# A tenth home for expert weight tiles, five experts a loop turn, earlier loads and a reordered first gather in a single-core MoE step

## The reference

```python
def moe_ffn(h, w_router, b_router, w_gu, b_gu, w_down, b_down):
    logits = h @ w_router + b_router              # 320 x 32
    top_val, top_idx = top_k(logits, 4)           # 4 of 32 experts a row
    gate = softmax(top_val)
    for e in range(32):                           # rows that chose expert e
        gu = x_e @ w_gu[e] + b_gu[e]              # w_gu[e]: 1024 x 2048 float32, 8 MiB
        gt, up = min(gu[:, :1024], 7), clip(gu[:, 1024:], -7, 7)
        act = gt * sigmoid(1.702 * gt) * (up + 1)
        y[rows] += gate * (act @ w_down[e] + b_down[e])   # w_down[e]: 1024 x 1024, 4 MiB
```

## Time and profile before

| | |
|---|---|
| median of 3 runs | 1288.66 us (1286.66 to 1289.59) |
| the profiled execution | 1286.78 us |
| its span, first to last instruction | 1285.0 us |
| PE busy | 98% of the span, 8556 matmul records |
| DVE, ACT busy | 36%, 16% |
| mean granted PE clock | 0.995 of full speed |
| read from HBM | 435 MB |

### The profile page before, as it was taken

The page is one execution under the profiler, slowest core; times in us unless marked ns, Lnnn a source line. Parts: engine busy times, 40 slices in busy tenths (PEclk is TensorE's granted clock), DMA queues, the critical chain, the costliest instruction groups (busy, mean ns, idle before and its releaser), DMA issues.

```text
span 1285.0 us, 20897 instructions
## 1 busy us (share of the span) xinstructions
PE 1254.3 (98%) x8556; PEld 574.0 (45%) x8556; DVE 459.5 (36%) x970; ACT 207.8 (16%) x547; POOL 18.2 (1%) x34
## 2 busy tenths in 40 slices
PE   8999999999999999999999999999999999999997
PEld 5677654576653333333333333343333334333332
DVE  4454334525572223333322332332232333222233
ACT  2542433623420000000000000000000000000000
POOL 0000001100000000000000000000000000000000
PEclk9999999999989999999999999999999999999999
DMA  9611011953089999999999999999999999999996
GB/s 311 254 66 67 2 30 26 322 251 145 4 358 429 427 426 430 427 429 427 429 427 429 427 429 428 429 428 429 428 429 427 429 427 429 427 429 427 430 427 266
DMA packets 48768, 439.06 MB, mean 342 GB/s; under 512 B 8677, under 2 KB 11213, under 8 KB 24058
## 3 DMA queue, kind: packets, MB, share of 16 engines
q1 hardware_dynamic: 48492, 438.32, 81.9%
q10 hardware_dynamic: 238, 0.20, 0.1%
HBM read 435.17 MB, written 3.33 MB: 341 GB/s over the span
## 4 chain that ended last, share of the span: by engine, by line
PE 80%; DMA 16%; ACT 1%; DVE 1%; issue 1%; SPq 0%; DVEq 0%; POOLq 0%; POOL 0%; ACTq 0%
PE bank L1092 78%; DMA weights<-in_w_gu 16%; PE bank L1095 2%; ACT scaled L639 1%; DMA x<-in_x_sample 1%; PE bank L1755 0%; DVE x L2509 0%; ACT weights L639 0%; ACT small_weights L639 0%; DVE scaled L1970 0%; ACT scaled L1020 0%; DVE x L2180 0%; DVE stats L2284 0%; DVE small_weights L2361 0%; DVEq L2545 0%
## 5 line engine op out<-in xcount | busy, mean ns | idle before, releaser
L2509 DVE SCALAR_TENSOR_TENSOR x<-bank,small_weights,x 128x512 f32<-128x512 f32 (+1 forms) x192 | 134.9, 744 | 598.5 <-PE bank L1092 598.5
L1092 PE MATMUL bank<-weights,small_weights 128*64 128x512 f32 x1360 | 308.7, 596 | 3.6 <-DMA weights<-in_w_gu 3.1
L1092 PEld LDWEIGHTS bank<-weights,small_weights 128*64 128x64 f32 x1360 | 92.4, 136 | 188.8 <-issue 170.2
L1092 PE MATMUL bank<-weights,scaled 128*64 128x512 f32 x704 | 155.9, 595 | 5.1 <-ACT scaled L639 5.1
L1092 PE MATMUL bank<-small_weights,weights 128*128 128x320 f32 (+4 forms) x400 | 110.0, 422 | 0.1
L1092 PE MATMUL bank<-scaled,small_weights 64*128 64x512 f32 x384 | 108.1, 640 | 1.4 <-DVE x L2509 0.7
L639 ACT ACTIVATE scaled<-scaled 128x512 f32<-128x512 f32 x32 | 20.1, 630 | 548.8 <-DVE scaled L1901 548.8
L639 ACT ACTIVATE scaled<-bank 128x512 f32<-128x512 f32 (+6 forms) x145 | 54.8, 406 | 325.8 <-PE bank L1092 244.7
L1092 PEld LDWEIGHTS bank<-weights,scaled 128*64 128x64 f32 x704 | 48.7, 137 | 97.1 <-issue 87.7
L1092 PE MATMUL bank<-stream,small_weights 128*64 128x512 f32 (+4 forms) x408 | 87.4, 544 | 1.5 <-DMA stream<-in_w_gu 1.1
L1092 PEld LDWEIGHTS bank<-stream 128*128 128x128 bf16 (+1 forms) x2416 | 75.0, 100 | 27.6 <-issue 26.4
(11 more groups left out here) (207 smaller groups left out, 879.8 us busy)
## 6 DMA issues: line engine op xcount, KB each, us to landing
weights<-in_w_gu SPq DMA_DIRECT2D x85, 2048.0 KB, 26.9
weights<-in_w_down SPq DMA_DIRECT2D x44, 2048.0 KB, 28.3
stream<-in_w_gu SPq DMA_DIRECT2D x21, 2048.0 KB, 28.1
more_weights<-in_w_gu SPq DMA_DIRECT2D x11, 2048.0 KB, 27.6
small_weights<-in_w_gu SPq DMA_DIRECT2D x11, 2048.0 KB, 26.2
small_weights<-in_w_down SPq DMA_DIRECT2D x10, 2048.0 KB, 28.2
more_weights<-in_w_down SPq DMA_DIRECT2D x10, 2048.0 KB, 28.4
weights<-in_w_in SPq DMA_DIRECT2D x3, 2048.0 KB, 14.0
```

Of the source, the lines that this page charges most:

```text
L1092: return pe.matmul(out, lhsT, rhs, start=start, stop=stop)
L2509: dve.scalar_tensor_tensor(xx, PS[bank][0:rows, :], gcur[0:rows, b:b + 1], xx, ALU.mult, ALU.add)\
```

## The change

- **Homes.** `SLOTN` becomes 10: two homes in `stream` (columns 3840 and 7936) in place of one, which takes smaller parts and tables there. 30 tiles are three times 10 homes, so `TURN` becomes 5, with six turns in place of ten.
- **Sample rows folded.** Block 2 of the residual is kept as `x3s`, 128 partitions x 512: partitions 0 to 63 hold the first half of the 64 rows, 64 to 127 the second. Its `x3_add`, its square, its parts, its `scatter` and its `accumulate` are one step of 512 columns in place of two half-filled ones (`HALVES` = 5 in place of 6 everywhere). A row's sum of squares then lies in two partitions; `sample_sum` (PE) adds them and `sample_rstd` (ACT) makes the norm. The router and the ranks of block 2 are computed for both halves of the partitions. A gather is 48 matmuls of 64 columns and 12 of 128.
- **Tables moved.** Masks, ranks, S and the lists move from `stream` to `small_weights`; the down bias to `gain_rows`; the raw bias, the router's weights and the small bfloat16 constants to `x`; the transposed rows for the router get a tile of their own, `x3T`; the memory attention's output `om` is split by row block.
- **First loads.** Four homes get their first tile on other conditions; the down bias is loaded and split with the gate-up bias.
- **The way to the first gather.** `x3_scale` goes: ACT makes the first part from `x3` with the norm as its scale, and `x3_rest` is a scale and subtract in one (two instructions). Masks are bfloat16, rank matmuls too. The ranks of blocks 0 and 1 have a bank and a mark (`rank01_mm`) of their own, `iota` starts at 1 so that one DVE operation less follows the ranks, and `slots` is two operations, `slots01` and `slots2`. `first_gather` does the 48 matmuls of blocks 0 and 1 when `slots01` is there, and block 2's afterwards. Gate sums are taken for all blocks at once.

The diff, cut to these parts:

```diff
@@ constants and homes
-        GT, TILES, SLOTN, TURN = 4, 6, 9, 3
-        slot_sb = [W[:, 4 * FF * n:4 * FF * (n + 1)] for n in range(6)] + [VK[:, 5888:9984], RH[:, 2816:6912], W2[:, :]]
+        GT, TILES, SLOTN, TURN = 4, 6, 10, 5
+        slot_sb = [W[:, 4 * FF * n:4 * FF * (n + 1)] for n in range(6)] + [VK[:, 3840:7936], RH[:, 2816:6912], W2[:, :], VK[:, 7936:12032]]
...
+        x3s, xs3s = X[:, 2 * D:2 * D + 512], XS[:, 2 * D:2 * D + 512]
+        HALVES = 2 * TB - 1
@@ SP
             for n in range(3):
                 load(braw[32 * n:32 * n + 32, :], b_gu[0], "ld_bias")
+            for n in range(3):
+                load(bdn[32 * n:32 * n + 32, :], b_down[0], "ld_bias")
...
             sp.wait_ge(sem("x2_mm"), KD)
+            first_tiles(TILES, TILES + 1)
+            sp.wait_ge(sem("x2_add"), KD)
+            first_tiles(8, 9)
+            sp.wait_ge(sem("b3_step"), 12)
             load(wr_sb, k_major(w_router[0], 0, KD), "ld_wr")
-            for n in range(3):
-                load(bdn[32 * n:32 * n + 32, :], b_down[0], "ld_wr")
-            sp.wait_ge(sem("x2_add"), KD)
-            first_tiles(SLOTN - 1, SLOTN)
             sp.wait_ge(*at("qm_mm"))
             first_tiles(0, 1)
-            sp.wait_ge(sem("x3_mm"), 2 * TB)
+            sp.wait_ge(sem("att_s"), ATT["mem"] + UNITS)
+            first_tiles(7, 8)
+            sp.wait_ge(sem("x3_mm"), HALVES)
             first_tiles(1, 2)
-            first_tiles(TILES, TILES + 1)
             sp.wait_ge(sem("lg_mm"), TB)
-            first_tiles(TILES + 1, SLOTN - 1)
+            first_tiles(9, 10)
@@ ACT
             def part(b, i):
-                act.wait_ge(sem("xs_ready"), 2 * b + i + 1)
-                run(xparts[:, b, i, :], xs3[:, b, :]).then_inc(sem("x3_part"), 1)
+                if i == 0:
+                    act.wait_ge(sem("x3_rstd"), 2 * b + 2)
+                    dst, src = (xparts[:, b, 0, :], x3[:, b, :]) if b < 2 else (sparts[:, 0, :], x3s)
+                    m = run(dst.rearrange("p (m i t) -> p m i t", i=2, t=P), src.rearrange("p (m t i) -> p m i t", t=P, i=2),
+                            scale=ssq[:, 8 + b:9 + b])
...
@@ PE
+            def sample_sum():
+                pe.wait_ge(sem("x3_sq"), TB)
+                for side in range(2):
+                    m = mm(PS[5][half(side), 0:1], eye2, ssq[:, 10:11])
+                m.then_inc(mark("pair_mm"), 1)
...
             rows_feature_major(2)
+            sample_sum()
             router(2)
...
             pe.wait_ge(*at("mask01_ready"))
-            for b, a in ((0, 0), (1, 0), (1, 1), (2, 0), (2, 1)):
-                ranks(b, a)
+            mm(PS[3][:, E:2 * E], onesb, mask[:, 0, :], True, False)
+            mm(PS[3][:, 0:E], ustrictb, mask[:, 0, :], False, False)
+            mm(PS[3][:, E:2 * E], ustrictb, mask[:, 1, :], False, True).then_inc(mark("rank01_mm"), 1)
+            for b in range(2):
+                mm(PS[6][:, 0:2 * E].rearrange("p (b e) -> p b e", b=2), onesb, bcast(mask[:, b, :], [P, 2, E], 1), b == 0, False)
             for b in range(2):
                 counts(b)
+            pe.wait_ge(sem("b3_step"), 12)
+            gate_up_bias(0)
             pe.wait_ge(*at("mask_ready"))
-            ranks(2, 2).then_inc(mark("rank_mm"), 1)
+            mm(PS[6][:, 0:2 * E], ustrictb, mask[:, 2:4, :], False, True).then_inc(mark("rank_mm"), 1)
...
                 pe.wait_ge(sem("slots_ready"), 1)
                 pe.wait_ge(sem("x3_part"), 4)
-                pe.wait_ge(sem("parts_ready"), 1)
-                gather_pass([(0, 0), (0, 1), (0, 2), (1, 0), (1, 1)], True, False)
+                pe.wait_ge(sem("parts_ready"), 2)
+                gather_pass(ALL_PARTS[0:6], True, False)
+                pe.wait_ge(sem("slots_ready"), 2)
                 pe.wait_ge(sem("x3_part"), 6)
-                gather_pass([(2, 0), (2, 1)], False, False)
+                gather_pass(ALL_PARTS[6:8], False, False)
                 pe.wait_ge(sem("parts_ready"), TB)
-                gather_pass([(1, 2), (2, 2)], False, True).then_inc(sem("gather_mm"), 1)
+                gather_pass(ALL_PARTS[8:9], False, True).then_inc(sem("gather_mm"), 1)
...
+                if b == 2:
+                    mm(PS[bank][:, :], slotT[:, 2 * P:3 * P], y_sb).then_inc(sem("scat_mm"), 1)
+                    return
@@ DVE
-            slots(0, None)
-            last_part(1)
+            dve.wait_ge(*at("rank01_mm"))
+            slot_ranks(0, 3)
+            slots01(0, iota[:, 0:SLOTS])
+            dve.wait_ge(*at("rank_mm"))
+            slot_ranks(2, 6)
+            slots2(0, iota[:, 0:SLOTS])
+            x3_rest(2)
```

More of the change, by code:

```diff
@@ L1061, in _ @@
             for b in range(TB):
-                rows = P if b < 2 else DEC
-                run(gate[0:rows, b, :], lg[0:rows, b, 0:E], ACT.Exp, bias=ntop[0:rows, b:b + 1]).then_inc(sem("gate_exp"), 1)
+                run(gate[:, b, :], lg[:, b, 0:E], ACT.Exp, bias=ntop[:, b:b + 1]).then_inc(sem("gate_exp"), 1)
             def sigmoid(it):
@@ L1685, in router @@
                         pe.wait_ge(sem("x3_ev"), 2 * b + 1 + k // 4)
-                    m = mm(PS[b][0:rows, 0:E], hT[:, k, b * P:b * P + rows], wr_sb[:, k, :], k == 0, k == KD - 1)
+                    if b < 2:
+                        m = mm(PS[b][:, 0:E], x3T[:, k, :], wr_sb[:, k, :], k == 0, k == KD - 1)
+                    else:
+                        for side in range(2):
+                            m = mm(PS[2][half(side), 0:E], x3T[:, k, 0:DEC], wr_sb[:, k, :], k == 0, k == KD - 1)
                 m.then_inc(sem("lg_mm"), 1)
@@ L1733, in gather_pass @@
             def gather_pass(terms, begin, end):
[L1735 removed]
+                for k in range(4):
                     for b, i in terms:
[L1737 to L1738 removed]
+                        first, last = begin and k == 0 and (b, i) == terms[0], end and k == 3 and (b, i) == terms[-1]
+                        if b == 2:
+                            m = mm(xg_pair[:, :, k, :], sparts[:, i, k * P:(k + 1) * P], S[:, 2, :, :], False, last)
+                            continue
+                        for kk in (k, k + 4):
+                            m = mm(PS[4][:, kk * SLOTS:(kk + 1) * SLOTS], xparts[:, b, i, kk * P:(kk + 1) * P], S[:, b, 0, :],
+                                   first and kk == k, last and kk > k)
                 return m
@@ L2447, in gates @@
             def gates():
                 dve.wait_ge(sem("gate_exp"), TB)
-                link(tt(gate, gate, mask, ALU.mult))
-                for b in range(TB):
-                    rows = P if b < 2 else DEC
-                    link(dve.tensor_reduce(gsum[0:rows, b:b + 1], gate[0:rows, b, :], AX, ALU.add))
-                    link(dve.reciprocal(gsum[0:rows, b:b + 1], gsum[0:rows, b:b + 1]))
-                    link(ts(gate[0:rows, b, :], gate[0:rows, b, :], gsum[0:rows, b:b + 1]))
-                dve.memset(KT[:, 1208:1209], 0.0).then_inc(mark("gate_ready"), 1)
+                tt(gate[:, 0:2, :], gate[:, 0:2, :], mask[:, 0:2, :], ALU.mult)
@@ L2458, in extra_starts @@
+                for side in range(2):
+                    m = tt(gate[half(side), 2, :], gate[half(side), 2, :], mask[half(side), 2 + side, :], ALU.mult)
+                link(m)
+                link(dve.tensor_reduce(gsum, gate, AX, ALU.add))
+                link(dve.reciprocal(gsum, gsum))
+                link(tt(gate, gate, bcast(gsum, [P, TB, E], 2), ALU.mult))
+                dve.memset(KT[:, 842:843], 0.0).then_inc(mark("gate_ready"), 1)
             def extra_starts():
@@ L2524, in _ @@
             extra_starts()
-            for i in range(6, 12):
-                bias_step(i, bdn, bd3)
             extra_list()
```

317 lines of the change are left out of this document (166 added, 151 removed).

## The result

| | before | changed |
|---|---|---|
| median | 1288.38 us (6 runs, 1286.66 to 1290.04) | 1295.4 us (6 runs, 1293.58 to 1296.06) |
| ratio | | 1.0053 [1.0043, 1.0063] |
| span of the profiled execution | 1285.0 us | 1294.1 us |
| first refill issued | 371.51 us | 373.18 us |
| last `down` starts | 1268.34 us | 1277.61 us |

The change is slower by 0.5%, where 1282.9 us was forecast; the time lies outside the range. In the changed program `mm` is line 1112, `transposes` 1115, ACT's `run` 643, `accumulate` 2560.

The account below looks back on a forecast made before the run. Weight transfers through full DMA engines were taken to set the end. Tenth home -4.9, way to first refill -0.4 and tail -0.5 sum to -5.8 us, giving 1282.9 us against the 1288.66 us median; range 1278.8 to 1286.3 us.

Parts of the forecast that it names:

- What bounds the kernel: Experts' loop: full DMA engines at 428 GB/s set the end, 4.89 us a weight tile, though PE is busy 98%.
- the tenth home: Weight buffers: ten tiles in place of nine are there when refills begin, one fewer to come, -4.9 us.
- The way to the first refill: Head, from block 2's mask through router, ranks, slots and first gather: -0.4 us, bounds +1.0 and -1.5.
- the doubled router: Head, block 2's router on PE: 32 records in place of 16, taken as +1.0 us.
- its sign of being wrong: First refill later than 372.5 us, a loop stretch under 425 GB/s, or PE setting the pace to the end.
- The pause of the DMA until the first refill: Head: with ten homes filled, DMA engines stand idle from 367 us to the first refill at some 371.
- The tail: After the experts: last accumulate has five steps for six, block 2 stored in two pieces; -0.5 us, bounds 0 and -0.7.
- 28.21 becomes some 27.5 us: PE's time an expert in the loop, from fewer gather records and a halved scatter pair; worth 0 as weights bind.
- the back-edge rival: Loop of five: PE stalls at five back-edges; 6.5 us each needed to be slower, 8 us gives some 1297; chance 0.04.
- 24 us to spare: PE's lead at its last tile wait, 1232 us against weights at 1256, at 27.5 us an expert; 4.8 us a back-edge.
- The loop of three shows none: Argument against back-edge stalls in the loop of five: the old three-expert turn shows no instruction-fetch stall.
- What the rows price is the transfer ... 1.4 us: Loop of five: a whole turn's instructions fetched again five times, 0.6 MB at 428 GB/s; kept for the range only.

Follow-up runs that it names:

- run 643: Not a follow-up run: ACT's `run` in the changed program's code, at source line 643; no time of its own is given.

## Why the prediction was wrong

| kernel of the change | packets | us |
|---|---|---|
| ten homes, turn of 3, in order | 28 | 1280.35 |
| nine homes, turn of 3 | 28 | 1286.74 |
| ten homes, written out | 66 | 1290.07 |
| ten homes, turn of 10 | 72 | 1290.67 |
| ten homes, turn of 5 (the change) | 75 | 1295.4 |

**What bounds the kernel: right** for before, and for the tenth home: -4.9 us forecast, 4.85, 5.0 and 5.0 measured in three pairs. With it the version in the first row reaches the forecast 1282.9 and passes it. (The 1035 us at which PE was said to begin waiting is where the row's window starts; the trace's first wait for a DMA over 0.15 us ends at 1080.5 us, and the chain's first DMA piece in the loop starts at 1046.32.)

**The way to the first refill: right in size, by luck**, -0.4 forecast and some -0.6 measured with nine homes. From the router of block 2 to the gather it became 1.4 us shorter, where 0.5 was forecast: the doubled router, taken at +1.0, cost nothing. The rest was given back where nothing was counted, 0.3 us between gather and first refill and 0.4 us ahead of the router. In the changed kernel's profile itself the first refill came at 373.18 us, later than the 372.5 that the forecast named as its sign of being wrong, and PE set the pace to the end, which was another. The pause of the DMA until the first refill came as forecast. **The tail: mis-sized**, -0.5 forecast; from last `down` to the end of the span it is 16.5 us against 16.7, though `accumulate` takes 3.38 in place of 4.05 us. What lies behind it there wasn't tried.

**"28.21 becomes some 27.5 us": wrong.** The step halved the scatter pair's time because one record does the work of two. The rows after show 1.12 us for two records as for four: the half-height records had run two at a time already. The gather's 12 records of twice the columns take as long as the 24 they replace. It was called worth 0, but the back-edge rival's "24 us to spare" rested on it. At 28.18 us PE is 0.68 x 30 = 20.4 us later: 3.6 us to spare, and the fastest kernel shows just that (with its first `down` at 384.49 us, 384.49 + 31 x 28.18 = 1258.1 us for the last one by PE's pace, 1261.7 by the weights). With 3.6 in place of 24, the point from which that rival decides is (3.6 + 5.8 + 2.6) / 5 = 2.4 us a back-edge, not 6.5.

**"The loop of three shows none" as evidence against a stall: wrong.** The back-edges cost PE 3.2 us each, in stops that end 1.6 to 1.7 us after an instruction packet has ended. The mechanism was described in the rival, its chance of 0.04 was the error: nothing in the rows of before could speak of a turn longer than theirs. The Trainium skill, "Runtime: NRT & Kernel Launch", section "Instruction fetch mechanics", says that a taken branch to a block outside the window stalls on a fetch. For turns of five, six and ten experts the traces agree, by the packets at the stops and the 75, 81 and 72 in all. It also says that the window is two blocks of 256 instructions; by that the turns of three and four (some 1,110 and 1,480) would be fetched anew, and 28 and 32 packets show that they are not.

**"What the rows price is the transfer ... 1.4 us": wrong.** 47 packets more came, as the forecast's own test had it (75), and a packet costs some 0.2 us, not 0.04. From the first row of the table to the turn of ten it is 10.3 us for 44 packets; from first refill to last `down` their profiles differ by 9.0 us. The same page of the Trainium skill says that a long kernel needn't fit and that crossing a block is mostly hidden. Hidden from PE it is: the written-out kernels show no "issue". But where the DMA engines are full, the weights pay.

So the change, against 1288.4 us: its homes and steps -8.0, the fetched packets some +10, the back-edges beyond the packets +5. The two prices overlap in one trace, since the later of weights and PE decides; only the kernels that keep one of them tell them apart.

**Left open:** on which engines instruction packets fall, and why one takes 1.07 us where a weight packet takes 0.61; why the added time of the five back-edges grows from 2.5 to 4.2 us; whether a stall is shorter when the DMA engines are idle. None of these was tried.

## What to carry to other kernels

Before you lengthen a loop's body, count its instructions on each engine: here some 1,480 on PE stayed and some 1,850 were fetched again each turn, and the page's packet count (28, 32, 75) tells it at once. Where DMA engines are full, instruction traffic and small reads are not free: price them by what one more of them cost in a run (here 0.2 us, and 0.6 for a one-row read), not by bytes over sixteen. And if a new number of buffers seems to force a longer turn, look for an assignment that keeps the turn, and load in order again before the buffers run empty.

## What was not expected of the hardware

- A straight line of instructions made a kernel slower than its loop: 1297.69 against 1288.7 us, with no wait of PE for instructions. A packet of instructions took its DMA engine 1.07 us, a packet of weights of the same size 0.61 us.
- One read of 16 KB into one partition cost the whole kernel 0.60 us each time; the same bytes over 16 partitions 0.20 us.
- A float32 product with 128 rows and 128 columns of weights took 1.12 us where two products with half the rows, run side by side, took 1.13 us together, so folding two half-filled steps into one full one saved DVE and ACT time, and none on PE.
